# Small products of a block inverse spread over two more quarters of TensorE's array

## The chip, the cores and the metric

The kernel runs on one NeuronCore of one Trainium2 chip. TensorE (PE) multiplies, VectorE (DVE), ScalarE (ACT) and GpSimd (POOL) do elementwise work, SyncE (SP) issues the loads. The metric is the device time of one execution, in microseconds (us), as the median of the runs.

## The reference, cut to what matters

One decoder layer over 256 tokens of width 2048: an input projection, sparse attention on one half of the heads and an RWKV-7 recurrence on the other 16 heads of 64, then an output projection, attention over 256 memory tokens and a mixture of experts. The change lies in the recurrence:

```python
def step(S, inp):
    r_t, w_t, k_t, v_t, kk_t, a_t = inp
    sa = jnp.einsum("bhij,bhj->bhi", S, -kk_t)
    S = (S * w_t[:, :, None, :] + sa[..., None] * (kk_t * a_t)[:, :, None, :]
         + v_t[..., None] * k_t[:, :, None, :])
    return S, jnp.einsum("bhij,bhj->bhi", S, r_t)
```

## The kernel before

**Chunks and blocks.** The recurrence is done in 4 groups (`g`) of 4 heads and 4 chunks (`c`) of 64 tokens. A chunk of a head needs the inverse of a 64x64 unit triangular matrix. Two heads lie side by side, one in partitions 0 to 63 and one in 64 to 127 (`HEADS`); `pi` is 0 or 1 for the two pairs of heads of a group. A block `k` (0 to 7) stands for one chunk and one `pi`, so that odd `k` is `pi` = 1. Every product is 64x64 fp32 and is issued once per partition half `r`: operands in half `r`, output in half `r`. It thus uses the two diagonal quarters of the 128x128 array only (rows 0-63 to columns 0-63, rows 64-127 to columns 64-127). One fp32 product is two records in the trace.

**The inverse.** `X[:, 0]` holds the inverses so far and `X[:, 1]` the same matrices turned. Five levels (`LV`) double the size of the solved blocks. At a level PE does P = AM X0 (L972, 16 products), ACT copies it to `Ps` (L1650), PE does the update of X0 (L982, 16 products, not at level 5) and of X1 (L987, 16 products), DVE adds them to `X` (L2154), and POOL masks `AM` for the next level (L2680). Behind level 1 stand the turned `BK` (`trb`, L998, 32 products by the identity), behind level 2 the turned `z` (`trv`, L1007, 16). P of a level waits for POOL's `AM` and for DVE's X0 sum of the level before; the updates wait for `Ps`.

**Before the levels** PE makes the Gram products (L947, L951; then L958), DVE masks them into `AB` (L2130) and makes X0 (L2135, L2136), POOL makes X1 and `AM` (L2685, L2686, L2680), and PE's P of level 1 waits for both.

**The chunks.** For each chunk in order: Z (L1022 from the second chunk on, L1025), ACT's copy `Zs` (L1666), U (L1032), DVE's copy `Us` (L2159), then the state S (L1040, L1043) and the output Y (L1049, L1053, L1056), both written out of `Us`.

**Fillers.** Between these steps PE runs a part of the big input projection: `gap()` issues the next few of a list `GAPS` of counts, each unit being three 128x128 matmuls with 256 columns (`product`, L843). The counts are fixed: 9 units behind the Gram products, `[3, 0] * 4 + [3, 2]` in the five levels (3 behind P, 0 behind the updates), 3 in each gap of the chunks. ACT (L1597) and DVE (L2023) prepare the weight pieces for them in their own `gap()`. The order on each engine is written out by hand; semaphores with named steps (`Progress`) tie the engines together.

Of the kernel before, what the change touches and what calls it, by code (L numbers as in the profile page):

```python
# [40 lines left out]
HEADS = (slice(0, CH), slice(CH, 2 * CH))  # L41
NGRP = 4
# [33 lines left out]
def decoder_layer(nc, x_in, mem, ln1_g, w_in, cmp_pos_k, cmp_w1_k, cmp_w2_k, cmp_pos_v, cmp_w1_v,  # L76
# [5 lines left out]
    with ctx:  # L82
# [248 lines left out]
        bank = [ctx.enter_context(nc.psum_tensor(f"bank{i}", [P, 512], F32)) for i in range(8)]  # L331
# [63 lines left out]
        class Chain:  # L395
# [5 lines left out]
            def __call__(self, ins):  # L401
# [18 lines left out]
               + [("X", g, 5, 1)] * (lv == 5) + {1: [("trb", g)], 2: [("trv", g)]}.get(lv, [])]  # L420
# [6 lines left out]
            + [k for lv in LV for k in [("Ps", g, lv)] + {1: [("trb", g)], 2: [("trv", g)]}.get(lv, [])]  # L427
# [3 lines left out]
            [("kx2", g), ("ssm", g), ("mix", g), ("kn", g), ("D", g), ("bon", g), ("hat", g), ("tI", g), ("G", g, 0),  # L431
             ("G", g, 1), ("AK", g)]
# [369 lines left out]
        def _(pe):  # L802
# [111 lines left out]
            for g in range(NGRP):  # L914
# [29 lines left out]
                for tt in range(NT):  # L944
                    for k, c, pi in pairs(tt):
                        for r in HEADS:
                            pe.matmul(b2(2 + 2 * tt, 4)[r, k, :].rearrange("p (a b) -> p a b", a=2),  # L947
                                      BK[r, 0, pi, chunk(c)], CR[r, pi, :, chunk(c)], start=True, stop=True)
                    for k, c, pi in pairs(tt):
                        for r in HEADS:  # L950
                            mm = pe.matmul(bank[5 + 2 * tt][r, k * CH:k * CH + CH], CR[r, pi, 0, chunk(c)],  # L951
                                           BK[r, 0, pi, chunk(c)], start=True, stop=True)
                    mm.then_inc(*pe_rw.mark(("G", g, tt)))
                pe.wait_ge(*dve_rw.at(("tI", g)))
                for tt in range(NT):
                    for k, c, pi in pairs(tt):
                        for r in HEADS:
                            mm = pe.matmul(b2(3 + 3 * tt, 4)[r, k, :].rearrange("p (a b) -> p a b", a=2),  # L958
# [4 lines left out]
                for lv in LV:  # L963
                    if lv == 1:
                        pe.wait_ge(*dve_rw.at(("G", g, 1)))
# [11 lines left out]
                    if lv > 1:  # L977
                        pe.wait_ge(*dve_rw.at(("X", g, lv - 1, 1)))
                    if lv < 5:
                        for k in range(8):  # L980
                            for r in HEADS:
                                mm = pe.matmul(b2(5, 8)[r, k, :], X[r, 1, k // 4, k % 4, :], Ps[r, k // 4, k % 4, :],  # L982
                                               start=True, stop=True)
# [7 lines left out]
                    if lv == 1:  # L991
                        pe.wait_ge(*dve_rw.at(("AK", g)))
                        for tt in range(NT):
                            for k, c, pi in pairs(tt):
                                for j in range(2):
                                    for r in HEADS:
                                        at = (2 * k + j) * CH
                                        mm = pe.matmul(bank[3 + 3 * tt][r, at:at + CH], BK[r, j, pi, chunk(c)],  # L998
                                                       ident[r, r], start=True, stop=True)
                        mm.then_inc(*pe_rw.mark(("trb", g)))  # L1000
                    if lv == 2:
                        pe.wait_ge(*act_rw.at(("trb", g)))
                        for c in range(NCH):
                            for pi in range(2):
                                for r in HEADS:
                                    at = (2 * c + pi) * CH
                                    mm = pe.matmul(bank[3][r, at:at + CH], z[r, 4 + pi, chunk(c)], ident[r, r],  # L1007
# [3 lines left out]
                for c in range(NCH):  # L1011
# [508 lines left out]
        def _(act):  # L1520
# [104 lines left out]
            for g in range(NGRP):  # L1625
# [1164 lines left out]
```

## Time and profile before

| | |
|---|---|
| median of 3 runs | 1537.63 us (1532.42 to 1537.74) |
| the profiled execution | 1536.5 us, its span 1534.7 us |
| PE busy | 1467.7 us, 96% of the span |
| DVE, ACT, POOL busy | 730.9, 511.1, 139.9 us |

The recurrent stage lies between about 98 us and 440 us of the span. Times in the rows are us from the start of the span. A row of a timeline gives the start, the length from the first start to the last end, the engine and line, the operation with its size, and how many instructions are merged in it.

### The profile page before, as it was taken

The numbers are of one execution on the slowest core, as the hardware profiler recorded it, in microseconds if no ns is written. First come the engines' busy times: TensorE is split into PE (matmuls) and PEld (weight loads), VectorE is DVE, ScalarE is ACT, GpSimd is POOL, SyncE is SP. The second block draws the span as 40 slices with busy tenths as digits, with TensorE's granted clock in tenths as the row PEclk, the third lists the DMA queues.
The fourth block names the chain that finished last, engine by engine and source line by source line (L and its number), as shares of the span: only waits on it lengthen the run. The fifth ranks groups of instructions, "written<-read, shape, count | busy, mean of one in ns | idle before, by whom it ended". The sixth has DMA issues, their size and how long they took to land.

```text
span 1534.7 us, 27424 instructions
## 1 busy us (share of the span) xinstructions
PE 1467.7 (96%) x11862; PEld 1127.8 (73%) x11862; DVE 730.9 (48%) x1287; ACT 511.1 (33%) x878; POOL 139.9 (9%) x263
## 2 busy tenths in 40 slices
PE   6999999999999999999999999999999989898997
PEld 6999998989989999999889997876333333333332
DVE  4583755738446655454545343555224224222425
ACT  5542423424235544554435333532111101010103
POOL 6010020200220000000000000011111110110100
PEclk9999999999999999999999999999999999999999
DMA  6642313315247455344663615674899999999996
GB/s 207 200 154 69 119 57 118 112 56 160 71 164 239 152 164 165 110 165 173 212 216 127 205 56 173 219 310 171 363 420 422 420 421 421 422 421 421 421 414 238
DMA packets 159614, 350.99 MB, mean 229 GB/s; under 512 B 13616, under 2 KB 111498, under 8 KB 135050
## 3 DMA queue, kind: packets, MB, share of 16 engines
q1 hardware_dynamic: 159498, 349.30, 61.6%
q8 instruction: 90, 1.47, 0.4%
q14 instruction: 26, 0.21, 0.0%
HBM read 347.18 MB, written 2.10 MB: 228 GB/s over the span
## 4 chain that ended last, share of the span: by engine, by line
PE 83%; DMA 7%; DVE 5%; issue 2%; ACT 1%; POOL 1%; SPq 1%; DVEq 0%; ACTq 0%
PE bank L843 20%; PE bank L1357 12%; PE bank L1197 11%; PE bank L838 8%; DMA expert_unit<-in_moe_w_down_dram 7%; PE bank L1217 6%; PE bank L1391 5%; PE bank L1433 3%; PE bank L972 1%; PE bank L987 1%; PE bank L982 1%; PE bank L1329 1%; PE bank L1242 1%; PE bank L1265 1%; DVE hidden_lo_chunks L2003 1%
## 5 line engine op out<-in xcount | busy, mean ns | idle before, releaser
L843 PE MATMUL bank<-hidden_lo_chunks,piece 128*128 128x256 f32 x928 | 263.3, 284 | 0.0
L1357 PE MATMUL bank<-expert_unit,pair_entries 128*64 128x512 f32 x1024 | 239.4, 611 | 24.4 <-issue 24.4
L1597 ACT CAST piece<-arena_fixed 128x1024 fp32r<-128x1024 f32 (+1 forms) x160 | 164.0, 1036 | 190.3 <-PE bank L843 149.1
L2023 DVE TENSOR_TENSOR piece<-arena_fixed,piece 128x1024 fp32r<-128x1024 f32 (+1 forms) x160 | 192.3, 1223 | 58.5 <-ACT piece L1597 58.0
L1357 PEld LDWEIGHTS bank<-expert_unit,pair_entries 128*64 128x64 f32 x1024 | 72.9, 140 | 163.4 <-issue 163.4
L843 PE MATMUL bank<-hidden_hi_high_chunks,piece 128*128 128x256 f32 x928 | 181.3, 293 | 2.7 <-DVE piece L2023 2.2
L843 PE MATMUL bank<-hidden_hi_low_chunks,piece 128*128 128x256 f32 x928 | 179.0, 291 | 0.2 <-DVE piece L2023 0.2
L843 PEld LDWEIGHTS bank<-hidden_lo_chunks,piece 128*128 128x128 f32 x928 | 178.7, 193 | 0.0
L2276 DVE TENSOR_TENSOR loop_split<-arena_fixed,loop_split 128x2048 fp32r<-128x2048 f32 x48 | 107.9, 2288 | 113.6 <-ACT loop_split L1765 113.6
L843 PEld LDWEIGHTS bank<-hidden_hi_high_chunks,piece 128*128 128x128 f32 x928 | 146.1, 194 | 9.4 <-issue 5.6
L843 PEld LDWEIGHTS bank<-hidden_hi_low_chunks,piece 128*128 128x128 f32 x928 | 143.8, 191 | 7.3 <-issue 4.2
L2532 DVE TENSOR_TENSOR arena_phases<-arena_phases,bank 128x512 f32<-128x512 f32 x128 | 81.8, 681 | 139.8 <-PE bank L1433 139.8
L1197 PE MATMUL bank<-loop_split,act_over_concat 128*128 128x512 f32 x384 | 130.1, 393 | 2.5 <-issue 2.5
L1890 ACT CAST down_hi_lo<-bank 128x512 fp32r<-128x512 f32 x64 | 37.5, 587 | 246.1 <-PE bank L1433 142.1
L1765 ACT CAST loop_split<-arena_fixed 128x2048 fp32r<-128x2048 f32 x48 | 89.8, 1929 | 88.7 <-PE bank L1197 60.1
L1391 PE MATMUL bank<-expert_unit,hidden_turned 128*64 128x512 f32 x512 | 114.1, 594 | 4.5 <-DMA expert_unit<-in_moe_w_down_dram 4.5
L2524 DVE TENSOR_TENSOR down_hi_lo<-bank,down_hi_lo 128x512 fp32r<-128x512 f32 x64 | 44.2, 690 | 112.0 <-ACT down_hi_lo L1890 112.0
L1391 PEld LDWEIGHTS bank<-expert_unit,hidden_turned 128*64 128x64 f32 x512 | 38.5, 137 | 75.2 <-issue 75.2
L1217 PE MATMUL bank<-act_over_concat,loop_split 128*128 128x256 f32 x512 | 93.0, 285 | 0.0
L838 PE MATMUL bank<-piece,hidden_lo_chunks 128*128 128x256 f32 x320 | 90.5, 283 | 0.0
L1197 PE MATMUL bank<-loop_split,act_over_hT 128*128 128x512 f32 x256 | 89.7, 391 | 0.0
L1197 PEld LDWEIGHTS bank<-loop_split,act_over_concat 128*128 128x128 f32 x384 | 72.8, 190 | 18.1 <-issue 2.9
(400 smaller groups left out, 2125.3 us busy)
## 6 DMA issues: line engine op xcount, KB each, us to landing
expert_unit<-in_moe_w_gate_dram SPq DMA_DIRECT2D x64, 1024.0 KB, 23.1
expert_unit<-in_moe_w_up_dram SPq DMA_DIRECT2D x64, 1024.0 KB, 25.9
expert_unit<-in_moe_w_down_dram SPq DMA_DIRECT2D x56, 1024.0 KB, 23.2
arena_fixed<-in_w_in_dram SPq DMA_DIRECT2D x23, 2048.0 KB, 9.2
arena_fixed<-in_wk_mem_dram SPq DMA_DIRECT2D x8, 2048.0 KB, 8.6
arena_fixed<-in_wv_mem_dram SPq DMA_DIRECT2D x8, 2048.0 KB, 8.2
arena_fixed<-in_w_out_dram SPq DMA_DIRECT2D x8, 2048.0 KB, 8.0
arena_fixed<-in_wq_mem_dram SPq DMA_DIRECT2D x8, 2048.0 KB, 8.3
```

The lines of the kernel that those rows point to most:

```text
L838: mm = pe.matmul(b[:, half * UC:half * UC + UC], hidden_x(x_, c)[:, half * P:half * P + P], w(w_)[:, k % 4, :], start=False, stop=r == 2 * ...
L843: mm = pe.matmul(b[:, half * T:half * T + T], w(w_)[:, k % 8, :], hidden_x(x_, c), start=c + t == 0, stop=c == NC - 1 and t == 2)
L1197: mm = pe.matmul(b, src(x_, cc)[:, half * P:half * P + P], lspl[2 * s + h][:, y_, c * WC:c * WC + WC], start=s + h + c + k == 0, stop=end)
L1217: mm = pe.matmul(b, lspl[2 * s + h][:, y_, at:at + P], src(x_, NC // 2 * h + c), start=h + c + k == 0, stop=h == 1 and c == NC // 2 - 1 an ...
L1357: mm = pe.matmul(bank[b][o, :].rearrange("p (g n) -> p g n", g=2), hs_pair[:, c, o], gate_up_unit(i(e))[:, :, c % (NC // 2), :], start=c = ...
L1391: mm = pe.matmul(bank[4 + q][o, :], tTs[:, turn, f, o], down_unit(i(e))[:, f, q * 512:q * 512 + 512], start=f == 0, stop=f == 1)
L1433: mm = pe.matmul(bank[b][:, :], Gt[:, turn, f % 2, :], osp[q % 2][:, half, :], start=half == 0, stop=half == 1)
L1597: nc.scalar.copy(piece_half(p, 0), raw_piece(p)).then_inc(piece_hi, 1)
L1765: nc.scalar.copy(lspl[2 * s + h][:, 0, :], slot(s)[:, h * HU:h * HU + HU]).then_inc(loop_hi, 1)
L2023: V.tensor_tensor(piece_half(p, 1), raw_piece(p), piece_half(p, 0).bitcast(F32), ALU.subtract)\
L2276: V.tensor_tensor(sl[:, 1, :], slot(s)[:, r:r + HU], sl[:, 0, :].bitcast(F32), ALU.subtract)\
L2532: return TT(xs, xs, bank[b][:, :], ALU.add)
```

## The change

For odd `k` (and `pi` = 1) the turned inverse `X[:, 1]`, `Ps` and `Zs` are kept in the other partition half. `SIDES[k % 2]` gives the pairs of input half and output half: for even `k` they are equal, for odd `k` crossed. So P, the X0 update, Z and U of odd blocks run in the two off-diagonal quarters; the X1 update, `trb`, `trv`, S and Y stay on the diagonal. Even and odd blocks write different PSUM banks, and the copies and sums read two banks through `two_banks` and write in the order `odd_even`. POOL makes the turned start only for even blocks; for odd ones PE makes the Gram product once more with its output crossed (8 products per group) and DVE masks it. DVE now makes X0 of all 8 blocks in one pair of operations instead of two. To free banks, `trb` is split into two halves of 16 products behind levels 1 and 2, and `trv` moves behind level 3. The lists of `Progress` follow and are left out here.

```diff
@@ -39,6 +39,7 @@
 CH = 64
 NCH = T // CH
 HEADS = (slice(0, CH), slice(CH, 2 * CH))
+SIDES = (tuple(zip(HEADS, HEADS)), tuple(zip(HEADS, HEADS[::-1])))
 NGRP = 4
 NSA_COLS = 2584
 RW = 1024
@@ -328,7 +329,14 @@
             return prm[:, i:i + 1]
 
 
-        bank = [ctx.enter_context(nc.psum_tensor(f"bank{i}", [P, 512], F32)) for i in range(8)]
+        banks = ctx.enter_context(nc.psum_tensor("banks", [P, 8, 512], F32))
+        bank = [banks[:, i, :] for i in range(8)]
+
+        def two_banks(i, n):
+            return banks[:, i:i + 2, 0:n].rearrange("p e (m c) -> p e m c", c=CH)
+
+        def odd_even(tile):
+            return tile.rearrange("p a b c -> p (a b c)").rearrange("p (m e c) -> p e m c", e=2, c=CH)
 
...
@@ -944,43 +954,51 @@
                 for tt in range(NT):
                     for k, c, pi in pairs(tt):
                         for r in HEADS:
-                            pe.matmul(b2(2 + 2 * tt, 4)[r, k, :].rearrange("p (a b) -> p a b", a=2),
+                            pe.matmul(b2(2 + tt, 4)[r, k, :].rearrange("p (a b) -> p a b", a=2),
                                       BK[r, 0, pi, chunk(c)], CR[r, pi, :, chunk(c)], start=True, stop=True)
                     for k, c, pi in pairs(tt):
                         for r in HEADS:
-                            mm = pe.matmul(bank[5 + 2 * tt][r, k * CH:k * CH + CH], CR[r, pi, 0, chunk(c)],
+                            at = (4 * tt + k) * CH
+                            mm = pe.matmul(bank[7][r, at:at + CH], CR[r, pi, 0, chunk(c)],
                                            BK[r, 0, pi, chunk(c)], start=True, stop=True)
+                        if pi:
+                            for r, o in SIDES[1]:
+                                at = (2 * tt + k // 2) * CH
+                                mm = pe.matmul(bank[5][o, at:at + CH], BK[r, 0, pi, chunk(c)],
+                                               CR[r, pi, 0, chunk(c)], start=True, stop=True)
                     mm.then_inc(*pe_rw.mark(("G", g, tt)))
                 pe.wait_ge(*dve_rw.at(("tI", g)))
                 for tt in range(NT):
                     for k, c, pi in pairs(tt):
                         for r in HEADS:
-                            mm = pe.matmul(b2(3 + 3 * tt, 4)[r, k, :].rearrange("p (a b) -> p a b", a=2),
+                            mm = pe.matmul(b2(4 + 2 * tt, 4)[r, k, :].rearrange("p (a b) -> p a b", a=2),
                                            BK[r, 1, pi, chunk(c)], CR[r, pi, :, chunk(c)], start=True, stop=True)
                 mm.then_inc(*pe_rw.mark(("AK", g)))
                 gap()
 
                 for lv in LV:
                     if lv == 1:
-                        pe.wait_ge(*dve_rw.at(("G", g, 1)))
+                        pe.wait_ge(*dve_rw.at(("X0", g)))
                         pe.wait_ge(*pool_rw.at(("AM", g, 1, 1)))
                     else:
                         pe.wait_ge(*pool_rw.at(("AM", g, lv)))
                         pe.wait_ge(*dve_rw.at(("X", g, lv - 1, 0)))
                     for k in range(8):
-                        for r in HEADS:
-                            mm = pe.matmul(b2(2, 8)[r, k, :], AM[r, k // 4, k % 4, :], X[r, 0, k // 4, k % 4, :],
-                                           start=True, stop=True)
+                        for r, o in SIDES[k % 2]:
+                            mm = pe.matmul(b2(2 + k % 2, 8)[o, k // 2, :], AM[r, k // 4, k % 4, :],
+                                           X[r, 0, k // 4, k % 4, :], start=True, stop=True)
                     mm.then_inc(*pe_rw.mark(("P", g, lv)))
                     gap()
                     pe.wait_ge(*act_rw.at(("Ps", g, lv)))
                     if lv > 1:
                         pe.wait_ge(*dve_rw.at(("X", g, lv - 1, 1)))
+                    else:
+                        pe.wait_ge(*dve_rw.at(("AK", g)))
                     if lv < 5:
                         for k in range(8):
-                            for r in HEADS:
-                                mm = pe.matmul(b2(5, 8)[r, k, :], X[r, 1, k // 4, k % 4, :], Ps[r, k // 4, k % 4, :],
...
@@ -988,23 +1006,24 @@
                                            start=True, stop=True)
                     mm.then_inc(*pe_rw.mark(("X", g, lv, 1)))
                     gap()
-                    if lv == 1:
-                        pe.wait_ge(*dve_rw.at(("AK", g)))
-                        for tt in range(NT):
-                            for k, c, pi in pairs(tt):
-                                for j in range(2):
-                                    for r in HEADS:
-                                        at = (2 * k + j) * CH
-                                        mm = pe.matmul(bank[3 + 3 * tt][r, at:at + CH], BK[r, j, pi, chunk(c)],
-                                                       ident[r, r], start=True, stop=True)
-                        mm.then_inc(*pe_rw.mark(("trb", g)))
-                    if lv == 2:
-                        pe.wait_ge(*act_rw.at(("trb", g)))
+                    if lv < 3:
+                        tt = lv - 1
+                        if tt:
+                            pe.wait_ge(*act_rw.at(("trb", g, 0)))
+                        for k, c, pi in pairs(tt):
+                            for j in range(2):
...
@@ -1016,20 +1035,21 @@
                     else:
                         pe.wait_ge(*dve_rw.at(("X", g, 5, 1)))
                         pe.wait_ge(*act_rw.at(("trv", g)))
+                    if c:
+                        for pi in range(2):
+                            for r, o in SIDES[pi]:
+                                pe.matmul(bank[2 + pi][o, 0:CH], CR[r, pi, 0, chunk(c)], Sc[r, pi, :],
+                                          start=True, stop=False)
                     for pi in range(2):
-                        if c:
-                            for r in HEADS:
-                                pe.matmul(bank[2][r, pi * CH:pi * CH + CH], CR[r, pi, 0, chunk(c)], Sc[r, pi, :],
-                                          start=True, stop=False)
-                        for r in HEADS:
-                            mm = pe.matmul(bank[2][r, pi * CH:pi * CH + CH], AK[r, tt, 2 * c2 + pi, 0, :],
+                        for r, o in SIDES[pi]:
+                            mm = pe.matmul(bank[2 + pi][o, 0:CH], AK[r, tt, 2 * c2 + pi, 0, :],
                                            Vt[r, c, pi, :], start=c == 0, stop=True)
                     mm.then_inc(*pe_rw.mark(("Z", g, c)))
                     gap()
                     pe.wait_ge(*act_rw.at(("Zs", g, c)))
                     for pi in range(2):
-                        for r in HEADS:
-                            mm = pe.matmul(bank[3][r, pi * CH:pi * CH + CH], X[r, 1, tt, 2 * c2 + pi, :], Zs[r, pi, :],
+                        for r, o in SIDES[pi]:
+                            mm = pe.matmul(bank[5 + pi][o, 0:CH], X[r, 1, tt, 2 * c2 + pi, :], Zs[r, pi, :],
                                            start=True, stop=True)
                     mm.then_inc(*pe_rw.mark(("U", g, c)))
                     gap()
@@ -1647,23 +1667,21 @@
                 gap()
                 for lv in LV:
                     act.wait_ge(*pe_rw.at(("P", g, lv)))
-                    nc.scalar.copy(Ps.rearrange("p a b c -> p (a b c)"), bank[2][:, :])\
+                    nc.scalar.copy(odd_even(Ps), two_banks(2, 4 * CH))\
                         .then_inc(*act_rw.mark(("Ps", g, lv)))
                     gap()
-                    if lv == 1:
-                        act.wait_ge(*pe_rw.at(("trb", g)))
-                        for tt in range(NT):
-                            ins = nc.scalar.copy(BKt[:, 2 * tt:2 * tt + 2].rearrange("p a b c d -> p (a b c d)"),
-                                                 bank[3 + 3 * tt][:, :])
-                        ins.then_inc(*act_rw.mark(("trb", g)))
-                    if lv == 2:
+                    if lv < 3:
+                        act.wait_ge(*pe_rw.at(("trb", g, lv - 1)))
+                        nc.scalar.copy(BKt[:, 2 * lv - 2:2 * lv].rearrange("p a b c d -> p (a b c d)"), bank[6][:, :])\
+                            .then_inc(*act_rw.mark(("trb", g, lv - 1)))
+                    if lv == 3:
                         act.wait_ge(*pe_rw.at(("trv", g)))
-                        nc.scalar.copy(Vt.rearrange("p a b c -> p (a b c)"), bank[3][:, :])\
+                        nc.scalar.copy(Vt.rearrange("p a b c -> p (a b c)"), bank[6][:, :])\
                             .then_inc(*act_rw.mark(("trv", g)))
                     gap()
                 for c in range(NCH):
                     act.wait_ge(*pe_rw.at(("Z", g, c)))
-                    nc.scalar.copy(flat(Zs), bank[2][:, 0:P]).then_inc(*act_rw.mark(("Zs", g, c)))
...
@@ -2131,12 +2149,16 @@
 
                 for tt in range(NT):
                     dve.wait_ge(*pe_rw.at(("G", g, tt)))
-                    masked(AB[:, tt], 2 + 2 * tt)
-                    link(V.tensor_tensor(X[:, 0, tt], b2(5 + 2 * tt, 8)[:, 0:4, :], bc(M0.unsqueeze(1), 4, CH), ALU.mult))
-                    V.tensor_tensor(X[:, 0, tt], X[:, 0, tt], bc(id64.unsqueeze(1), 4, CH), ALU.add)\
-                        .then_inc(*dve_rw.mark(("G", g, tt)))
+                    masked(AB[:, tt], 2 + tt).then_inc(*dve_rw.mark(("AB", g, tt)))
+                inverse = X[:, 0].rearrange("p a b c -> p (a b) c")
+                link(V.tensor_tensor(inverse, b2(7, 8), bc(M0.unsqueeze(1), 8, CH), ALU.mult))
+                V.tensor_tensor(inverse, inverse, bc(id64.unsqueeze(1), 8, CH), ALU.add)\
+                    .then_inc(*dve_rw.mark(("X0", g)))
+                turned = odd_even(X[:, 1])[:, 1]
+                link(V.tensor_tensor(turned, b2(5, 8)[:, 0:4, :], bc(MTk[:, 0, :].unsqueeze(1), 4, CH), ALU.mult))
+                V.tensor_tensor(turned, turned, bc(id64.unsqueeze(1), 4, CH), ALU.add)
                 dve.wait_ge(*pe_rw.at(("AK", g)))
-                masked(AK[:, 0], 3)
+                masked(AK[:, 0], 4)
                 masked(AK[:, 1], 6).then_inc(*dve_rw.mark(("AK", g)))
                 dve.wait_ge(*dve_rw.at(("AK", g)))
                 gap()
@@ -2150,13 +2172,18 @@
                             dve.wait_ge(*dve_rw.at(("X", g, lv - 1, i)))
                         elif i:
                             dve.wait_ge(*pool_rw.at(("X0", g, 1)))
-                        o = X[:, i].rearrange("p a b c -> p (a b c)")
-                        V.tensor_tensor(o, o, bank[5 + 2 * i][:, :], ALU.add).then_inc(*dve_rw.mark(("X", g, lv, i)))
+                        if i == 0:
+                            o = odd_even(X[:, 0])
+                            ins = V.tensor_tensor(o, o, two_banks(4, 4 * CH), ALU.add)
+                        else:
+                            o = X[:, 1].rearrange("p a b c -> p (a b c)")
+                            ins = V.tensor_tensor(o, o, bank[7][:, :], ALU.add)
+                        ins.then_inc(*dve_rw.mark(("X", g, lv, i)))
                     gap()
                 for c in range(NCH):
                     gap()
                     dve.wait_ge(*pe_rw.at(("U", g, c)))
-                    V.tensor_copy(flat(Us), bank[3][:, 0:P]).then_inc(*dve_rw.mark(("Us", g, c)))
+                    V.tensor_copy(Us, banks[:, 5:7, 0:CH]).then_inc(*dve_rw.mark(("Us", g, c)))
                     gap()
                     if c < NCH - 1:
                         dve.wait_ge(*pe_rw.at(("S", g, c)))
@@ -2681,9 +2708,11 @@
                                             bc(MTk[:, lv, :].unsqueeze(1), n, CH), ALU.mult)
 
                 for tt in range(NT):
-                    pool.wait_ge(*dve_rw.at(("G", g, tt)))
-                    link(G_.tensor_tensor(X[:, 1, tt], AB[:, tt, :, 0, :], bc(MTk[:, 0, :].unsqueeze(1), 4, CH), ALU.mult))
-                    G_.tensor_tensor(X[:, 1, tt], X[:, 1, tt], bc(id64.unsqueeze(1), 4, CH), ALU.add)\
+                    pool.wait_ge(*dve_rw.at(("AB", g, tt)))
+                    kept = X[:, 1, tt].rearrange("p (b e) c -> p b e c", e=2)[:, :, 0, :]
+                    source = AB[:, tt].rearrange("p (b e) j c -> p b e j c", e=2)[:, :, 0, 0, :]
+                    link(G_.tensor_tensor(kept, source, bc(MTk[:, 0, :].unsqueeze(1), 2, CH), ALU.mult))
+                    G_.tensor_tensor(kept, kept, bc(id64.unsqueeze(1), 2, CH), ALU.add)\
                         .then_inc(*pool_rw.mark(("X0", g, tt)))
                     level(1, tt, tt + 1).then_inc(*pool_rw.mark(("AM", g, 1, tt)))
                 for lv in LV[1:]:
```

## Rows read from the trace of the kernel before

**Rows 1.** The page: span, busy time, granted clock and DMA in 40 slices.
```profile
span 1534.7 us, 27424 instructions
...
PE 1467.7 (96%) x11862; PEld 1127.8 (73%) x11862; DVE 730.9 (48%) x1287; ACT 511.1 (33%) x878; POOL 139.9 (9%) x263
...
PEclk9999999999999999999999999999999999999999
DMA  6642313315247455344663615674899999999996
```

**Rows 2.** Busy time in stretches of the first group: levels, then chunks.
```profile
106.00:132.00 26.00, 25.35 (x604) 23.72 (x604) 10.54 (x14) 8.23 (x12) 6.41 (x5) 1.00 0.27 85
132.00:155.00 23.00, 23.00 (x330) 20.73 (x331) 8.27 (x14) 6.33 (x10) 0.00 (x0) 1.00 0.29 93
```

**Rows 3.** Waits of PE from 90 to 425 us: total, times, longest.
```profile
PE bank L972 <- POOL arena_phases L2680: 1.3, 4, 0.4
PE bank L1007 <- issue: 0.6, 1, 0.6
PE bank L998 <- issue: 0.4, 1, 0.4
PE bank L972 <- issue: 0.4, 1, 0.4
```

**Rows 4.** Chain that ended last, levels 3 and 4 of the first group.
```profile
119.03 0.93 PE bank L972 x32
119.96 1.27 PE bank L843 x9
121.23 1.08 PE bank L982 x32
122.31 0.93 PE bank L987 x32
123.25 1.10 PE bank L972 x32
```

**Rows 5.** Timeline, engines beside PE at level 3.
```profile
120.01 0.59 ACT L1650 COPY arena_phases<-bank 128x512 f32<-128x512 f32 x1 [0.35 <-PE bank L972]
...
122.36 0.69 DVE L2154 TENSOR_TENSOR arena_phases<-arena_phases,bank 128x512 f32<-128x512 f32 x1 [3.53 <-PE bank L982]
```

**Rows 6.** Timeline of PE in the second chunk and behind the first.
```profile
136.05 0.28 PE L1056 MATMUL bank<-arena_phases 64*64 64x64 f32 x4
136.26 0.50 PE L843 MATMUL bank<-hidden_hi_low_chunks,piece 128*128 128x256 f32 x2
...
137.81 0.28 PE L1022 MATMUL bank<-arena_phases 64*64 64x64 f32 x4
137.93 0.28 PE L1025 MATMUL bank<-arena_phases 64*64 64x64 f32 x4
```

**Rows 7.** Timeline: full array, row halves, column quarters, column halves.
```profile
13.81 0.94 PE L863 MATMUL bank<-norm_diagonals,tokens 128*128 128x128 f32 x7
...
78.30 0.48 PE L922 MATMUL bank<-arena_phases 64*128 64x256 f32 x1
...
78.31 0.48 PE L925 MATMUL bank<-arena_phases 64*128 64x256 f32 x1
...
474.67 1.96 PE L1089 MATMUL bank<-arena_phases,compress_blocks 128*32 128x128 f32 x64
...
1056.61 3.65 PE L1357 MATMUL bank<-expert_unit,pair_entries 128*64 128x512 f32 x16
```

**Rows 8.** Timeline of POOL and DVE before level 1, first group.
```profile
103.84 0.64 POOL L2685 TENSOR_TENSOR arena_phases<-arena_phases 128x256 f32<-128x256 f32 x1
105.15 1.62 POOL L2680 TENSOR_TENSOR arena_phases<-arena_phases 128x256 f32<-128x256 f32 x1
...
103.30 1.27 DVE L2130 TENSOR_TENSOR arena_phases<-bank,arena_phases 128x512 f32<-128x512 f32 x2
104.61 4.38 DVE L2023 TENSOR_TENSOR piece<-arena_fixed,piece 128x1024 fp32r<-128x1024 f32 x3
```

More of the change, by code:

```diff
@@ L419, in decoder_layer @@
             + [k for lv in LV for k in [("P", g, lv), ("X", g, lv, 0), ("X", g, lv, 1)][:None if lv < 5 else 1]
-               + [("X", g, 5, 1)] * (lv == 5) + {1: [("trb", g)], 2: [("trv", g)]}.get(lv, [])]
+               + [("X", g, 5, 1)] * (lv == 5)
+               + {1: [("trb", g, 0)], 2: [("trb", g, 1)], 3: [("trv", g)]}.get(lv, [])]
             + [k for c in range(NCH) for k in
@@ L426, in decoder_layer @@
             [("sq1", g), ("th", g), ("exp", g)]
-            + [k for lv in LV for k in [("Ps", g, lv)] + {1: [("trb", g)], 2: [("trv", g)]}.get(lv, [])]
+            + [k for lv in LV for k in [("Ps", g, lv)]
+               + {1: [("trb", g, 0)], 2: [("trb", g, 1)], 3: [("trv", g)]}.get(lv, [])]
             + [("Zs", g, c) for c in range(NCH)] + [("ys", g), ("sq2", g)]])
@@ L430, in decoder_layer @@
             k for g in range(NGRP) for k in
-            [("kx2", g), ("ssm", g), ("mix", g), ("kn", g), ("D", g), ("bon", g), ("hat", g), ("tI", g), ("G", g, 0),
-             ("G", g, 1), ("AK", g)]
+            [("kx2", g), ("ssm", g), ("mix", g), ("kn", g), ("D", g), ("bon", g), ("hat", g), ("tI", g), ("AB", g, 0),
+             ("AB", g, 1), ("X0", g), ("AK", g)]
             + [("X", g, lv, i) for lv in LV for i in range(2) if lv < 5 or i]
@@ L978, in _ @@
                         pe.wait_ge(*dve_rw.at(("X", g, lv - 1, 1)))
+                    else:
+                        pe.wait_ge(*dve_rw.at(("AK", g)))
                     if lv < 5:
                         for k in range(8):
-                            for r in HEADS:
-                                mm = pe.matmul(b2(5, 8)[r, k, :], X[r, 1, k // 4, k % 4, :], Ps[r, k // 4, k % 4, :],
-                                               start=True, stop=True)
+                            for r, o in SIDES[k % 2]:
+                                mm = pe.matmul(b2(4 + k % 2, 8)[o, k // 2, :], X[r, 1, k // 4, k % 4, :],
+                                               Ps[r, k // 4, k % 4, :], start=True, stop=True)
                         mm.then_inc(*pe_rw.mark(("X", g, lv, 0)))
@@ L990, in _ @@
                     gap()
-                    if lv == 1:
-                        pe.wait_ge(*dve_rw.at(("AK", g)))
-                        for tt in range(NT):
-                            for k, c, pi in pairs(tt):
-                                for j in range(2):
-                                    for r in HEADS:
-                                        at = (2 * k + j) * CH
-                                        mm = pe.matmul(bank[3 + 3 * tt][r, at:at + CH], BK[r, j, pi, chunk(c)],
-                                                       ident[r, r], start=True, stop=True)
-                        mm.then_inc(*pe_rw.mark(("trb", g)))
-                    if lv == 2:
-                        pe.wait_ge(*act_rw.at(("trb", g)))
+                    if lv < 3:
[4 more added lines that the diff above has]
+                            for j in range(2):
+                                for r in HEADS:
+                                    at = (2 * k + j) * CH
+                                    mm = pe.matmul(bank[6][r, at:at + CH], BK[r, j, pi, chunk(c)],
+                                                   ident[r, r], start=True, stop=True)
+                        mm.then_inc(*pe_rw.mark(("trb", g, tt)))
+                    if lv == 3:
+                        pe.wait_ge(*act_rw.at(("trb", g, 1)))
                         for c in range(NCH):
@@ L1006, in _ @@
                                     at = (2 * c + pi) * CH
-                                    mm = pe.matmul(bank[3][r, at:at + CH], z[r, 4 + pi, chunk(c)], ident[r, r],
+                                    mm = pe.matmul(bank[6][r, at:at + CH], z[r, 4 + pi, chunk(c)], ident[r, r],
                                                start=True, stop=True)
@@ L1649, in _ @@
                     act.wait_ge(*pe_rw.at(("P", g, lv)))
-                    nc.scalar.copy(Ps.rearrange("p a b c -> p (a b c)"), bank[2][:, :])\
+                    nc.scalar.copy(odd_even(Ps), two_banks(2, 4 * CH))\
                         .then_inc(*act_rw.mark(("Ps", g, lv)))
                     gap()
-                    if lv == 1:
-                        act.wait_ge(*pe_rw.at(("trb", g)))
-                        for tt in range(NT):
-                            ins = nc.scalar.copy(BKt[:, 2 * tt:2 * tt + 2].rearrange("p a b c d -> p (a b c d)"),
-                                                 bank[3 + 3 * tt][:, :])
-                        ins.then_inc(*act_rw.mark(("trb", g)))
-                    if lv == 2:
+                    if lv < 3:
+                        act.wait_ge(*pe_rw.at(("trb", g, lv - 1)))
+                        nc.scalar.copy(BKt[:, 2 * lv - 2:2 * lv].rearrange("p a b c d -> p (a b c d)"), bank[6][:, :])\
+                            .then_inc(*act_rw.mark(("trb", g, lv - 1)))
+                    if lv == 3:
                         act.wait_ge(*pe_rw.at(("trv", g)))
-                        nc.scalar.copy(Vt.rearrange("p a b c -> p (a b c)"), bank[3][:, :])\
+                        nc.scalar.copy(Vt.rearrange("p a b c -> p (a b c)"), bank[6][:, :])\
                             .then_inc(*act_rw.mark(("trv", g)))
@@ L1665, in _ @@
                     act.wait_ge(*pe_rw.at(("Z", g, c)))
-                    nc.scalar.copy(flat(Zs), bank[2][:, 0:P]).then_inc(*act_rw.mark(("Zs", g, c)))
+                    nc.scalar.copy(Zs, banks[:, 2:4, 0:CH]).then_inc(*act_rw.mark(("Zs", g, c)))
                     gap()
```

## The prediction

> **What bounds the kernel now.** I read the page first: PE is busy for 96% of the span at a granted clock of nine tenths or more in every slice [rows 1], and the table of stretches says the same of the stage that the change touches: in the levels of the first group PE was busy for 25.35 of 26.00 us, in its chunks for 23.00 of 23.00, at clock 1.00 with DMA at 0.27 to 0.29 [rows 2]. The list of PE's waits in the stage is short: 1.3 us on POOL in four times, once per group, and 1.4 us of "issue" in three pieces, in which PE had no instruction to run and nothing released it [rows 3]. So whatever time PE saves in this stage shortens the stage, as long as its partners stay ahead. In the chain of waits the levels are a row of PE pieces with nothing between [rows 4].
>
> What holds a burst of small products is seen in the same chain: 32 records (16 products) take 0.93 us [rows 4], 0.029 us per record, and the 4 of L1022 in the chunks took 137.93 - 137.81 = 0.12 us [rows 6], again 0.03. Only two quarters work, so each quarter takes one record per 0.058 us.
>
> **Do quarters that share rows or columns run side by side?** The trace has no off-diagonal quarter. It has each kind of sharing by itself [rows 7]. Row halves under the same columns: L922 (rows 0-63) has 4 records in program order before L925's (rows 64-127), and yet the first of L925 starts at 78.31, 0.01 us behind the first of L922; they write the same partitions in different banks, as the change's even and odd blocks do. Column parts that share all rows: L1089 uses four column parts of 32 and has 64 records of 128 columns in 1.96 us, 0.031 each, where the full array needed 0.94 / 7 = 0.13 each for as many columns (L863). L1357 uses two column parts: 16 records of 512 columns in 3.65 us, 0.23 each, where four times L863's would be 0.54. So both kinds of neighbours overlap fully, and each part keeps a queue of its own that a later instruction for another part passes. I take it that the four quarters run together: 8 records in each quarter at 0.058, thus 0.465 us per burst of 32.
>
> **What is saved on PE, per group.**
> - P: 5 levels, X0 update: 4 levels. 9 bursts x (0.93 - 0.465) = 4.19 us. The X1 update, `trb` (its 32 products only split 16 and 16) and `trv` keep their time.
> - Z: 8 records in the first chunk, 16 in the other three, U: 8 in each of four. At half the time that is 0.116 + 3 x 0.233 + 4 x 0.116 = 1.28 us.
> - Sum 5.47 us, in four groups 21.9 us.
>
> **The extra products.** The 8 crossed Gram products of a group stand behind others of the diagonal in the same burst. Run side by side they cost nothing, since the diagonal quarters have twice their work; run one behind the other they cost 16 records x 0.029 = 0.46 us per group, 1.9 in all. I take nothing, with the choice above.
>
> **Waits that change.** POOL's start of the levels gets shorter: its two operations per half drop from 256 to 128 elements, 0.64 us each now [rows 8]; four operations at about half save some 1.3 us per group, more than the 0.3 that PE waited. DVE's part grows: the old order took two masked sums more of 256 elements on POOL, now two more on DVE (0.41 to 0.76 us each by the neighbouring rows, so at most 1 us more before the AK pair at 103.30). It needs X0 only by the end of the fillers at 106.6, some 3 us after it. So the wait of 1.3 us goes [rows 3]. Behind it DVE has three pieces queued, 4.38 us from 104.61 [rows 8]; a start 1 us later ends them at 110.0, and the first X0 sum of the earlier PE would be due at about 109.3. It would be 0.7 us late, but PE has the X1 update and `trb` behind that (1.86 us), so P of level 2 is not held. If that cover were gone it would cost 0.7 x 4 = 3 us.
>
> At level 3 P of level 4 follows the X1 update directly and takes 1.10 instead of 0.93 [rows 4]: it waits 0.17 us for DVE's X0 sum (0.69 us, from 122.36) [rows 5]. `trv` moves into that place and covers it: 0.17 x 4 = 0.7 us gained. Level 4 keeps its wait.
>
> **Waits that could come.** A shorter P brings nobody closer to its deadline, for ACT's copy starts when P ends: 0.59 us at 120.01, done at 120.60, and the 9 fillers last until the update starts at 121.16 [rows 5, 4]; 0.56 us of slack remain. Should the copy of two banks in the new order be slower, the first half microsecond of it is free; a copy of 1.2 us would cost 0.05 us at each of 20 levels, 1 us. DVE's X0 sum has the X1 update beside it, which keeps its 0.93. POOL's mask has P to P less 0.93 us, about 3.2 us, for at most 1.8. The `trb` copy of ACT lies ahead of its next `Ps` copy: about 0.6 us of copy beside a P of 0.47 us delays `Ps` by 0.13, inside the slack.
>
> **Instruction supply.** The three "issue" waits [rows 3] fell where dense bursts of small products followed each other. Two of four bursts in a row now run in half the time, so an instruction that comes late is missed by up to 0.46 to 0.93 us more: 0 to 3 x 0.93 = 2.8 us for the three, and at the worst one new wait of 0.5 us at each of the 20 levels, 10 us. I take 2 us, near the lower end, because the bursts between fillers did not run dry elsewhere.
>
> **Sum.** 21.9 + 1.3 + 0.7 - 2 = 21.9 us off. The profiled execution took 1536.5 us; it gives 1514.6. That execution was 1.1 us under the median of the runs shown. What follows the stage moves up with it: the expert loads at the end fill the DMA engines in the last slices [rows 1], but their buffers are freed by PE's earlier stages, so they start earlier too. Its own range: 1507 (no new issue waits, the old ones gone, and 0.2% of scatter) to 1523 (10 us of supply waits).
>
> **Rivals.**
> *Shared rows, no overlap.* If a quarter must wait for the other quarter in its rows, bursts stay at 0.93, the crossed Gram products cost 1.9 us, and 1.3 + 0.7 are gained: 1536.4, no change. L1089 speaks against it, since its four parts share all rows. The Trainium skill (TensorE: Matmul & The Clock Gate, "Part 3: Packing small matmuls — row/col tiling") says that a weight load overlaps with running matmuls only when its row group differs, which would be this case. By that rule the time would be 1536; the trace does not agree with it for L1089, where 64 weight loads and matmuls went through in 1.96 us.
>
> *A limit on the rate of records.* If PE cannot start records faster than it did at its densest here, L1089's (1.96 - 0.27) / 63 = 0.027 us, a burst falls from 0.93 to 0.86 only, 8% of 21.9 us plus 2.0: 1532.7. That L1089 ran at this rate is explained by its 128 columns in four parts, so nothing needs such a limit; and L922 and L925 started 0.01 us apart. The Trainium skill (same page, "Wait — 56ns, not 53.3ns?") gives about 25 ns as the least distance from start to start however small the product. By it the burst would be 0.80 us and the time about 1531.5. The trace shows pairs of starts closer than that, but no longer run of them.
>
> *Changing between diagonal and crossed quarters costs a drain.* This is the one that ends slower. Where PE goes from small products to full ones it starts the next record 136.26 - 136.05 = 0.21 us after a group of four (0.12 without a change) [rows 6], so 0.09 us are lost. If each step from an even to an odd block cost that, a burst with 7 such steps would lose 0.63 us. Per group 9 x 7 steps in P and X0, some 21 in the Gram products, Z and U, 84 in all: 7.6 us, four groups 30 us, against 2 us of gained waits: 1565. It ends slower than before by 0.5% from 0.03 us per step upward, if nothing overlaps. Against it: four column parts alternate in L1089 from record to record at full rate.
>
> **How the numbers follow.** Four quarters together 0.76 (1514.6), shared rows 0.09 (1536.4), rate limit 0.08 (1532), drain 0.07 (1565). 0.5% of 1537.6 is 7.7 us, about what a measurement of this kernel can tell from no change; the bound of faster is 1529.9. So faster 0.76, same 0.17, slower 0.07. The range runs from 1507 to 1533: it holds nearly all of the first case and the rate limit, together 0.82.
>
> **What the next profile would show.** Bursts of P and of L982's successor at 0.47 us for 32 records (right) or 0.93 (shared rows), 0.80 to 0.86 (rate limit), 1.5 (drain); the X1 update unchanged at 0.93; the Gram burst unchanged in spite of more records; no wait of P on POOL at level 1, none on DVE at level 4; waits of "issue" between 1.4 and 11 us; PE busy about 20 us less in the first 440 us. The prediction is wrong if bursts do not shrink, if the update waits for `Ps`, or if DVE's first sum holds P of level 2.

## The result and the profile after

The changed kernel takes 1517.29 us (median of 4 runs, 1515.94 to 1518.91) against 1536.66 us of the kernel before; the ratio is 0.9887 (95% interval 0.9875 to 0.9899; it is not the quotient of these two medians, which is 0.9874). The prediction was 1514.6 us, range 1507 to 1533. The profiled execution took 1517.8 us. One run of those below, the sixth of "Loads from level 5 on", took 2355.97 us at a mean granted clock of 0.556, where its five others had 0.984 to 0.987, and its ratio leaves it out.

The page of the changed kernel, against [rows 1]:

```profile
span 1516.0 us, 27556 instructions
...
PE 1451.8 (96%) x11926; PEld 1107.7 (73%) x11926; DVE 731.1 (48%) x1287; ACT 511.1 (34%) x878; POOL 134.8 (9%) x263
...
PEclk9999999999999999999999999999999999999998
```

PE has 64 records more (the crossed Gram products) and is busy 15.9 us less; the span is 18.7 us shorter. DVE and ACT were busy for as long as before (within 0.2 us), so the copies over two banks cost nothing.

The chain of waits of the first group (start, length, piece), against [rows 4]. L988 is P, L1000 the X0 update, L1005 the X1 update, L1017 `trb`, L1026 `trv`, L853 the fillers:

```profile
106.57 0.62 PE banks L988 x32
107.20 1.27 PE banks L853 x9
108.47 0.62 PE banks L1000 x32
109.09 0.92 PE banks L1005 x32
110.01 0.93 PE banks L1017 x32
111.03 0.69 PE banks L988 x32
...
115.94 2.40 issue
118.34 0.21 PE banks L988
118.56 2.01 PE banks L853 x9
120.56 1.06 PE banks L1000 x32
121.62 1.23 PE banks L1005 x32
```

An update burst that took 1.08 us now takes 0.62, a saving of 0.46. The X1 update, still on the diagonal, keeps 0.92. At 115.94 PE stood for 2.40 us with nothing to run. Behind that wait everything on PE is slower, the 9 fillers 2.01 instead of 1.27 us. The table of stretches says why (last columns: granted clock, DMA share, GB/s):

```profile
116.00:118.50 2.50, 0.16 (x2) 0.02 (x1) 0.00 (x0) 0.11 (x1) 0.00 (x0) 1.00 0.71 235
118.50:121.00 2.50, 2.50 (x30) 2.27 (x33) 0.00 (x0) 2.12 (x3) 1.09 (x1) 0.55 0.05 14
121.00:123.00 2.00, 2.00 (x68) 2.00 (x64) 0.79 (x2) 0.00 (x0) 0.00 (x0) 0.71 0.00 0
```

After 2.5 us of hardly any PE work the granted clock was 0.55 for 2.5 us, close to the lower of its two levels (1.2 GHz, 0.50). The slow pieces are 0.74 + 0.44 + 0.31 = 1.5 us longer than their like: wait and slow stretch together cost 3.9 us, not 2.4. That the one brought the other was seen this once. Waits of 1.0 to 1.6 us (at 205 and 385 us here, and in the experiments) had no slow stretch behind them, and in this profile the clock was also at its lower level from 333.8 to 337.2 us, where PE had not stood still.

The waits of PE from 90 to 425 us, against [rows 3]:

```profile
PE banks L1005 <- issue: 2.5, 2, 1.5
PE banks L988 <- issue: 2.4, 1, 2.4
PE banks L913 <- DVE arena_phases L2202: 0.6, 1, 0.6
PE banks L1052 <- ACT arena_phases L1684: 0.3, 1, 0.3
```

The four waits on POOL are gone; "issue" grew from 1.4 to 4.9 us. The wait of 2.4 us is the largest at its place: in the four experiments below whose loads also run beside the first group's levels it was 0.7 us with everything on the diagonal and 1.4 to 1.6 us in the other three.

Lengths of the parts, from the first record of one part (weight loads included) to the first of the next in the two timelines, one number per group (us). "The mean" is the product behind the last chunk, L1061 before and L1081 after:

| part | before | after |
|---|---|---|
| first Gram product to P of level 1 | 8.32, 8.48, 8.33, 8.32 | 7.99 each |
| P of level 1 to Z | 25.00, 24.97, 24.32, 25.19 | 24.41, 21.26, 19.99, 22.05 |
| Z to the mean | 23.29, 23.29, 23.55, 23.29 | 22.10, 22.10, 22.47, 22.10 |

Only the levels differ from group to group. The third group has no wait of "issue" in its levels in either kernel and fell by 4.33 us; the others lost part of that, or, in the first group, nearly all of it.

### The profile page after: what moved, and what is told of

It is laid out like the page before. It is cut to its first block, busy times and chain, and to the rows that moved or that the text cites. A ratio compares the mean times of both kernels' runs of the same rounds, so it can differ in the third digit from the quotient of the medians.

```text
span 1516.0 us, 27556 instructions
## 1 busy us (share of the span) xinstructions
PE 1451.8 (96%) x11926; PEld 1107.7 (73%) x11926; DVE 731.1 (48%) x1287; ACT 511.1 (34%) x878; POOL 134.8 (9%) x263
## 4 chain that ended last, share of the span: by engine, by line
PE 87%; DMA 6%; DVE 3%; issue 2%; ACT 1%; SPq 0%; DVEq 0%; ACTq 0%
PE banks L853 23%; PE banks L1377 13%; PE banks L1217 11%; PE banks L848 8%; PE banks L1237 6%; PE banks L1411 6%; DMA expert_unit<-in_moe_w_down_dram 5%; PE banks L1453 3%; PE banks L1005 1%; PE banks L1349 1%; PE banks L1262 1%; PE banks L1285 1%; DVE hidden_lo_chunks L2021 1%; PE banks L988 1%; PE banks L1180 1%
## 5 line engine op out<-in xcount | busy, mean ns | idle before, releaser
L1377 PE MATMUL banks<-expert_unit,pair_entries 128*64 128x512 f32 x1024 | 244.5, 623 | 23.1 <-issue 23.1
L853 PE MATMUL banks<-hidden_lo_chunks,piece 128*128 128x256 f32 x928 | 264.5, 285 | 0.0
L853 PE MATMUL banks<-hidden_hi_high_chunks,piece 128*128 128x256 f32 x928 | 181.5, 294 | 2.7 <-DVE piece L2041 2.2
L853 PE MATMUL banks<-hidden_hi_low_chunks,piece 128*128 128x256 f32 x928 | 180.9, 293 | 0.2 <-DVE piece L2041 0.2
L853 PEld LDWEIGHTS banks<-hidden_lo_chunks,piece 128*128 128x128 f32 x928 | 179.7, 194 | 0.0
L853 PEld LDWEIGHTS banks<-hidden_hi_high_chunks,piece 128*128 128x128 f32 x928 | 146.2, 194 | 12.0 <-issue 8.3
L853 PEld LDWEIGHTS banks<-hidden_hi_low_chunks,piece 128*128 128x128 f32 x928 | 145.4, 193 | 7.6 <-issue 4.5
L1217 PE MATMUL banks<-loop_split,act_over_concat 128*128 128x512 f32 x384 | 128.9, 390 | 0.6 <-issue 0.6
L1411 PE MATMUL banks<-expert_unit,hidden_turned 128*64 128x512 f32 x512 | 113.9, 594 | 2.2 <-DMA expert_unit<-in_moe_w_down_dram 2.2
L1237 PE MATMUL banks<-act_over_concat,loop_split 128*128 128x256 f32 x512 | 92.3, 283 | 0.0
```

Source lines behind the costliest of these rows:

```text
L853: mm = pe.matmul(b[:, half * T:half * T + T], w(w_)[:, k % 8, :], hidden_x(x_, c), start=c + t == 0, stop=c == NC - 1 and t == 2)
L1217: mm = pe.matmul(b, src(x_, cc)[:, half * P:half * P + P], lspl[2 * s + h][:, y_, c * WC:c * WC + WC], start=s + h + c + k == 0, stop=end)
L1237: mm = pe.matmul(b, lspl[2 * s + h][:, y_, at:at + P], src(x_, NC // 2 * h + c), start=h + c + k == 0, stop=h == 1 and c == NC // 2 - 1 an ...
L1377: mm = pe.matmul(bank[b][o, :].rearrange("p (g n) -> p g n", g=2), hs_pair[:, c, o], gate_up_unit(i(e))[:, :, c % (NC // 2), :], start=c = ...
L1411: mm = pe.matmul(bank[4 + q][o, :], tTs[:, turn, f, o], down_unit(i(e))[:, f, q * 512:q * 512 + 512], start=f == 0, stop=f == 1)
```

## Experiments

**All on the diagonal.** Everything else of the change stays, one line is edited:

```diff
-SIDES = (tuple(zip(HEADS, HEADS)), tuple(zip(HEADS, HEADS[::-1])))
+SIDES = (tuple(zip(HEADS, HEADS)), tuple(zip(HEADS, HEADS)))
```

> The changed kernel with every product back on the two diagonal quarters; all its other edits stay (two banks per product group, X0 masked at once, the turned start of odd blocks made by extra Gram products, trb in two halves). Theory 1, the four quarters run together and that is the gain: the bursts of P and of the X0 update go from 0.62 us back to 1.08 us, Z and U as well, the 8 extra Gram products cost 0.46 us per group, so the stage is 4 x (9 x 0.46 + 1.2 + 0.46) = 23 us longer, less some of the instruction waits: 1536 to 1541 us. Theory 2, the gain came from the moved operations of DVE and POOL and from trb and trv behind other levels: it stays at 1517 to 1520 us.

Measured 1531.5 us (10 runs), ratio to the kernel before 0.9979 (0.9968 to 0.9989). Its chain of waits:

```profile
107.12 1.08 PE banks L988 x32
108.20 1.27 PE banks L853 x9
109.47 1.08 PE banks L1000 x32
110.55 0.93 PE banks L1005 x32
```

The bursts are back at 1.08 us, Z to the mean at 23.29, and the Gram part is 8.46, so the 8 extra products cost 0.47 us per group where they do not overlap. Theory 1 holds: the crossing is the gain. The time is 5 us below the expectation, and the parts say why. The levels take 25.01, 24.59, 24.15 and 24.15 us. From the first Gram product to the last mean this kernel is 15.4 us longer than the changed one: 1.9 in the Gram parts, 10.2 in the levels, 4.6 in the chunks, less 1.3 between the groups. The levels of the changed kernel hold 87.71 - 4 x 19.99 = 7.7 us of losses and these only 97.90 - 4 x 24.15 = 1.3 us. Without them the difference would be 23 us, as the expectation's sum has it; it named the instruction waits and took too little off for them. The 1.3 us between the groups are a stretch at the lower clock, which the changed kernel has at 333.8 us and this one does not.

**Even blocks first.** P and the X0 update in another order:

```diff
-                    for k in range(8):
+                    for k in (0, 2, 4, 6, 1, 3, 5, 7):
```

> The changed kernel with P and the X0 update issued as blocks 0, 2, 4, 6 and then 1, 3, 5, 7, so that 16 records for the diagonal quarters stand ahead of the first for a crossed one. If each quarter has a queue that later instructions reach at once, the bursts stay at 0.62 us and the time at 1517 us. If records start in program order except for a few, the two halves of a burst run one behind the other: bursts of about 1.08 us, 36 x 0.46 = 17 us more, 1534 us. A lookahead in between gives a time in between.

Measured 1520.6 us (4 runs), 0.9905 (0.9888 to 0.9923). The bursts lie between both theories:

```profile
106.56 0.91 PE banks L988 x30
107.46 1.27 PE banks L853 x9
108.73 0.73 PE banks L1000 x24
```

P takes 0.91 us. In the records the first crossed matmul starts when 10 of the 16 diagonal ones have started; the 4 weight loads and 6 matmuls between, which had not started, are about what PE sees ahead. So a quarter's work starts out of order, but over a short distance.

**Two even, two odd.** The same edit with the order 0, 2, 1, 3, 4, 6, 5, 7.

> The changed kernel with P and the X0 update in the order 0, 2, 1, 3, 4, 6, 5, 7. With four even blocks first the crossed quarters began when 10 of the 16 diagonal records had started, and a burst took 0.91 us. If PE sees some 10 instructions past those that have started, a crossed quarter now begins after 2 records per diagonal quarter at most and the burst takes 0.62 to 0.75 us, the time 1517 to 1519 us. If even and odd blocks must alternate for any overlap, 0.85 to 1.08 us and 1525 us or more.

Measured 1516.3 us (two runs), ratio 0.9881 (0.9853 to 0.9909), not to be told from the changed kernel's 0.9887. P took 0.67 us and the update nearly its 0.62:

```profile
106.53 0.67 PE banks L988 x30
107.20 1.26 PE banks L853 x9
```

Eight records ahead still fit into what PE sees. Strict alternation is not needed.

**Loads behind the levels.** The load queue waits before four of the 2 MB weight loads:

```diff
+            late = {9: 0, 13: 1, 18: 2, 22: 3}
             for n in range(2, NW):
+                if n in late:
+                    sp.wait_ge(*pe_rw.at(("Z", late[n], 0)))
                 load(n)
```

> The changed kernel with the four weight loads that fell into the levels (units 9, 13, 18, 22) held on the load queue until Z of the group's first chunk. Theory 1, PE runs out of instructions where a fetch of its next instructions stands behind the packets of a 2 MB load: the three waits of 'issue' (4.9 us, 2.4 the longest) and the stretch at half clock behind the longest (about 1.5 us) go, 1511 to 1513 us. Theory 2, the bursts are too dense for the supply whatever the DMA engines do: the waits stay at 4 to 6 us and the time at 1517 us. If ACT then waits for a late load, PE waits for Zs or Us in the chunks and the time rises.

Measured 1510.57 us (5 runs), 0.9841 (0.9822 to 0.9860). The list of PE's waits in the stage has no "issue" left; P to Z is 20.31, 19.99, 19.99 and 20.30 us. A new wait came, as the expectation feared:

```profile
PE banks L1044 <- DVE arena_phases L2198: 1.3, 1, 1.3
```

The second group's load was late; ACT stood before its cast (3.49 us, on the DMA) and DVE behind ACT.

**The same on the kernel before.**

> The kernel before with the same four loads held until Z of the group's first chunk. Theory 1, fetch behind a load: its three 'issue' waits (1.4 us) go and the time falls by 1 to 2 us, 1535 us. Theory 2, density alone: no change, 1536.7 us, with the waits still there.

Measured 1531.44 us (10 runs), 0.9979 (0.9969 to 0.9988), 3.7 us less than the 1535.16 us of the kernel before that was timed beside it. The levels take 24.32 to 24.33 us in all four groups, which were 24.32 to 25.19, and the same late load costs it 1.2 us:

```profile
PE bank L975 <- POOL arena_phases L2683: 1.3, 4, 0.4
PE bank L1025 <- DVE arena_phases L2171: 1.2, 1, 1.2
```

So the levels gave 2.2 us, just above the 1 to 2 us expected, and the late load took 1.2 back. The rest of the 3.7 us is not settled for the medians. The two profiles show one cause that has nothing to do with the loads: the kernel before was at the lower clock for 3.4 us at 26.4 and again at 347.2 us, and this one was not. Its first Gram product comes 1.55 us earlier and the part around the second stretch is 1.33 us shorter. Such stretches fall in different places from profile to profile, so a us or two between two kernels can be theirs.

**Loads from level 5 on.** The changed kernel again, with `("P", g, 5)` in place of `("Z", g, 0)`.

> The changed kernel with weight loads 9, 13, 18 and 22 held until P of level 5 of their group instead of until Z. In the run with Z the second group's load came so late that ACT and DVE stood behind it and PE waited 1.3 us for the state. Theory 1, fetch behind a load is what empties PE: the levels keep no wait of 'issue' over 0.3 us, since little dense work is left behind level 5, and the 1.3 us go: 1508 to 1510 us. Theory 2, density of the bursts: waits come back, since the loads are again within the levels, 1511 to 1514 us.

Measured 1510.99 us (5 runs; 1511.33 with the sixth), 0.9847 (0.9827 to 0.9866). The time does not tell the theories apart, for it lies between their ranges; the waits do. Those of PE in the stage are down to two, neither of "issue":

```profile
PE banks L916 <- DVE arena_phases L2205: 0.6, 1, 0.6
PE banks L1055 <- ACT arena_phases L1687: 0.3, 1, 0.3
```

The 1.3 us went; against the version with Z the two medians cannot be told apart. Where the instruction fetches are can be seen in the DMA view from 109.5 to 115.8 us, just ahead of the 2.40 us wait, first of the changed kernel. The first line is the busy share of the DMA engines in 40 slices:

```profile
DMA  0000000000039659998999999999999999999999
...
q1 hardware_dynamic: 1388, 1.42, 73.3%
```

The load starts at 111.2 us, and in the 4.6 us from there no packet of the instruction queue (q8, 16 KB each) got through. The next one started at 115.9 us, 9.4 us behind the first P of the group, was moved in 1.15 us, and PE went on 1.3 us after that. With the load held the packet starts at 112.0 us, 6.6 us behind the first P, so the load made it 2.8 us late:

```profile
DMA packets 1, 0.02 MB, mean 3 GB/s; under 512 B 0, under 2 KB 0, under 8 KB 0
...
q8 instruction: 1, 0.02, 1.0%
```

Each wait of "issue" of 0.3 us or more in the levels, in every profile that has one, ended 1.2 to 1.5 us behind the end of such a packet. A packet itself took 0.9 to 1.5 us with or without a load beside it, so what comes late is its start.

**A load put into the quiet group.** The changed kernel with unit 17 alone held until `("P", 2, 1)`.

> The changed kernel with one load moved, unit 17, held until P of level 1 of the third group, whose levels had no wait of 'issue' (19.99 us from the first P to Z). Theory 1, fetch behind a load: a wait of 0.6 to 2.5 us comes up in that group and its levels take 21 to 24 us; the other groups stay. Theory 2, density alone: the third group stays at 19.99 us.

Measured 1518.5 us (two runs). The third group's levels went from 19.99 to 21.85 us, in the chain:

```profile
291.81 0.35 PE banks L991 x19
292.16 1.54 issue
293.70 0.45 PE banks L991 x11
```

The second and fourth stayed within 0.1 us (21.25, 22.10); the first took 22.38 instead of 24.41 for a shorter wait there (1.6 us, against 2.4) without a slow stretch behind it, in a place that this edit does not touch: that much is scatter between executions. The whole time, 1518.5 us, cannot be told from the changed kernel's. The wait is made and unmade by the place of a load, so it is the load and not density alone. It still takes a dense stretch as well: no run had such a wait in the chunks, where fillers are the larger part, and in the third group of the changed kernel a load ran from 300.1 us on, beside level 5, without one.

## Why the prediction was right

**The four quarters** run together: 0.46 us saved per burst, 0.465 predicted. The absolute 0.47 held for the P bursts behind `trb` and `trv`. A burst behind fillers takes 0.15 us more in both kernels (1.08 and 0.62), so there the difference holds and the 0.47 did not. The levels of the third group, without instruction waits, fell by 24.32 - 19.99 = 4.33 us, predicted 4.19 + 0.17. The 0.17, P of level 4 that no longer waits for DVE, shows by itself with everything on the diagonal, where a level part without waits takes 24.15 us.

**Z and U** gave 1.19 us per group, predicted 1.28.

**The extra Gram products** cost nothing beside the others: from the first Gram product to L974 are 2.67 us, as before; on the diagonal they cost 0.47.

**The wait on POOL** went: 0.33 + 0.49 + 0.34 + 0.32 = 1.48 us, predicted 1.3.

**DVE's longer part** held something up, which the prediction had ruled out. It set DVE's 0.7 us of lateness against a cover of 1.86 us and left out that the sum itself takes 0.69 us, so the margin was 0.5 us and not 1.2. Then DVE came 0.2 us later and PE 0.2 us earlier than reckoned. In the first group:

```profile
105.89 4.39 DVE L2041 TENSOR_TENSOR piece<-arena_fixed,piece 128x1024 fp32r<-128x1024 f32 x3
110.21 0.68 DVE L2177 TENSOR_TENSOR arena_phases<-arena_phases,banks 128x512 f32<-128x512 f32 x1
```

The sum ends at 110.89 us, the halved `trb` at 110.94, and P of level 2 starts at 111.03 and takes 0.69 us instead of 0.47: 0.3 us lost. The fourth group loses the same, the other two nothing, where DVE has two pieces queued and not three. The runs with held loads, which have no "issue" in the levels, show it plainly: 20.31, 19.99, 19.99 and 20.30 us. So this sign of being wrong came up, at 0.6 us in all against the 3 us that the prediction had named as its price.

**Instruction supply** is the term that was mis-sized. "I take 2 us, near the lower end" measured 4.9 us: the instruction waits, with the slow stretch, cost the levels 87.71 - 80.59 = 7.1 us in the changed kernel and 99.48 - 97.30 = 2.2 us in the kernel before (each time the four level parts, less those with the loads held). With DVE's 0.6 us that closes the sum: 4 x 4.33 + 4.65 + 1.48 = 23.4 us of gains, less 5.5, are the 17.9 that the stage gained. I had taken the wait as a matter of density. It is a fetch that comes late beside a load. That denser bursts use up sooner what PE still holds, and so make the wait longer, fits 0.7 us with everything on the diagonal against 1.4 to 2.4 us crossed at the same place, but is argued from these few waits. With the loads held in both kernels the change is worth 1531.4 - 1510.6 = 20.9 us, where the prediction's sum without its supply term has 23.9; two late loads of 1.2 to 1.4 us, one in each, cancel in this.

**Behind the stage** the gain is carried through: 17.9 us at its end, 18.7 at the end of the span. The total is within 3 us of the forecast and hides no large errors: against the sum, the quarters gave 0.6 us less (21.3 of 21.9), DVE took 0.6 and the supply 2.9 us more, POOL gave 0.2 us more, and another 0.8 us came behind the stage. PE's busy time fell by 15.9 us and not by about 20.

**The rivals.** Shared rows without overlap and a rate limit fall with the bursts of 0.62 us, whose crossed records share rows with the diagonal ones beside them. Read record by record, the starts of a round of four lie 0.007 us apart and the next round follows 0.038 us behind the fourth, 0.0585 for each round: 0.0146 us per record. The Trainium skill (TensorE: Matmul & The Clock Gate, "Wait — 56ns, not 53.3ns?") gives about 25 ns as the least distance from start to start; this kernel's 32 records are below it on average, and three of four steps are 7 ns. The Trainium skill's rule (same page, "Part 3: Packing small matmuls — row/col tiling") that weight loads overlap only across row groups would, by an estimate, leave the bursts at 1.08 us; it does not hold here. The sum of the rate limit had a slip: 21.9 us are what halving the bursts saves, so 8% of a burst are 8% of twice that, 3.3 us with the rows' numbers, and the rival's time would be 1531.2, not 1532.7 us; with bursts of 0.80 us it would be 1528.4, not 1531.5. The low end of the range is also 1 us lower than its own items give (1536.5 - 23.9 - 1.4 - 3.1 = 1508.1). Neither changes the outcome. The drain rival fell too: the step from a diagonal to a crossed record within a round is 0.007 us. The Trainium skill (TensorEngine Tiling (Array Packing), "Key Properties") says a drain belongs to a change of the tiling mode and not of the tile, and the trace agrees with its second half.

## What to carry to other kernels

Products of 64x64 that leave half the array's quarters idle can be doubled up by letting every second operand live in the other partition half; write them to different banks and keep the four quarters' instructions within some ten of each other. When a stretch of PE becomes denser in instructions, look for waits of "issue" and keep big loads away from it: here four waits on the load queue were worth 6 to 7 us, a third of what the change itself brought. And when another engine takes over work, add the length of its next operation to its lateness before calling a wait covered.

## What the runs showed of the hardware

Four quarters reach 0.0146 us per record, two 0.029. PE starts the work of another quarter past about ten instructions that have not started (0.91 us against 0.62 for a burst). Beside a 2 MB load a fetch of instructions started late: none in 4.6 us, and then one 2.8 us later than with the load held (9.4 against 6.6 us behind the group's first P). A PE that stood still for 2.4 us for it was then granted 0.55 of its clock for 2.5 us, seen once; behind waits up to 1.6 us that did not happen.
